# One decoder layer on one core: four score blocks placed one weight half later, and the first extraction placed inside a gate half

## The chip, the cores and the metric

The kernel runs on one core of a Trainium2 chip. The metric is the device time of one execution in microseconds (us), and less is better. Five engines work side by side, each through its own list of instructions in order: TensorE (PE; its weight loads are listed apart as PEld), VectorE (DVE), ScalarE (ACT), GpSimd (POOL) and SyncE (SP). They meet only through semaphores. SP and POOL also issue most of the transfers (DMA) from memory.

## The reference

One layer is computed for a prompt of 256 tokens and for 8 sample sequences of one token each, in float32, so that there are 264 columns of activations. In short:

```python
x = x + 0.5 * g1 * swiglu(mod1(rms_norm(x)))
proj = mod2(rms_norm(x)) @ w_in            # qA kA vA | qB kB vB | gA | gB
o_a = block-sparse attention, 8 heads x 64 (prompt, and samples over a paged cache of 1024 tokens)
o_b = differential attention, 4 heads, q/k halves of 64, value 128 (the same, with a second cache)
x = x + g2 * ((sigmoid(gA) * (o_a @ w_branch_moba) + sigmoid(gB) * (rms_norm(o_b) @ w_branch_diff)) @ w_out)
x = x + 0.5 * g3 * swiglu(mod3(rms_norm(x)))
```

The shifts, scales and gates (mod1 to mod3, g1 to g3) come from a product of a conditioning vector with `w_ada`. The new rows of keys and values are returned too.

## The kernel before

**Products.** Every float32 weight block of 1 MB lands in one of four slots `raw`. ACT cuts it into a high part `whi` (line 773), and DVE (line 1147) or POOL (line 723) computes the rest `wlo`. PE then runs three products for each 128 by 128 piece of weights: high by high, high by low, low by high, each over 264 columns. A block of 256 output columns is worked in two halves, and one half is 8 pieces, so 24 products. The halves of the key and value projection are numbered; `kv_product(u)` (lines 1729 to 1731) is half u. Halves 0 to 15 are keys and values, halves 16 to 19 are the first two gate blocks. The later gate blocks are worked by `gate_half` (lines 2103 to 2105), whose result lies in PSUM bank 3.

**Scores.** The sample queries need scores against two caches, A (moba) and B (diff). `scores(ab, u)` (line 2003) multiplies the queries with half a sequence of cache `ab`: 32 small matmuls. Before it, the half must have landed in a buffer (1 MB, four transfers, line 493; SP issues those of A, POOL those of B) and must have been transposed in place by DVE (`turn_keys`, line 1378). A buffer is free again when its scores are done. For B, load 15 goes where load 12 was, load 16 (already the values of the first sequence) where load 13 was, load 17 where 14 was and load 18 where 15 was. POOL works in this order, and waits at each load for the scores that free its buffer:

```python
for use in range(KVS + 2, 4 * TS):
    kv_load(pool, 1, use)
    ...
    if 11 <= use < POOL_HALVES - 1:
        lo(*filler(use))       # wlo of weight half `use`
```

**The loop over u on PE.** Step u does `kv_product(u)`, then turns earlier keys or values (`k_turn`, `k_back`, `v_turn`; a value half is turned by line 1938 after ACT has copied it to `vT`, line 940), then `scores(0, u + 2)` and `scores(1, u)`. DVE in the same order transposes the halves of both caches; behind the last of them, `turn_keys(1, 15)`, come the ranks of the first four sequences (`sample_ranks(0)`, lines 1435 to 1460), and on these waits the exponential on ACT (line 955). Behind that exponential ACT copies value half 15 for `v_turn` of step 16, and then cuts the weights of halves 18 and 19.

**After the loop.** PE does halves 17 to 19 and then eight steps c. In step c it multiplies the probabilities (`wpad`, written by ACT at line 1041) with the cached values (line 2138), turns the prompt's probabilities (line 2168), computes the next prompt scores (lines 2054 and 2055), and does the prompt's output (lines 2192 and 2193). In steps 1 to 6 there are two gate halves between these. After step 3 and after step 7 the sample outputs of four sequences are complete in banks 4 and 5. DVE masks them into `om` (line 1604), and PE extracts them: eight matmuls of `om` with the 4 columns of the constant `sel4` (line 2200). Each is recorded as two passes with a weight load of 128 by 128 each.

Of the kernel before, what the change touches and what calls it, by code (L numbers as in the profile page):

```python
# [23 lines left out]
P = 128  # L24
D = 1024
KC = D // P
TP = 256
TS = 8
# [15 lines left out]
ADAS = (NMOD * D + ADAW - 1) // ADAW  # L44
KVS = 3
GUEST_LAST = 8
FIRST_LAST = 10
GATE_GUEST = 18
BIG = 1e30
# [165 lines left out]
def build(nc, A, O):  # L215
    ctx = ExitStack()
    with ctx:
# [1503 lines left out]
        def _(pe):  # L1721
# [334 lines left out]

            for u in range(2 * TS + 1):
                kv_product(u)
                if 1 <= u < 17:
                    kind, i = kv_half(u - 1)  # L2060
                    if kind == "k":
                        k_sum(i)
                    else:
                        v_turn(u - 1, i)
                if 2 <= u < 18:
                    kind, i = kv_half(u - 2)
                    if kind == "k":
                        k_turn(u - 2, i)
                if 3 <= u < 19:
                    kind, i = kv_half(u - 3)  # L2070
                    if kind == "k":
                        k_back(i)
                if u == 5:
                    pe.wait_ge(s_nvar, 3)
                if u == 13:
                    pe.wait_ge(s_ecur, 1)
                    pe.wait_ge(s_kroot, 8)
                    for r4 in range(4):
                        ins = mm(bank[:, 4, r4:r4 + 1], ev0[:, r4, :], C("ones", 0, 1), start=True, stop=True)
                    ins.then_inc(s_cur, 1)  # L2080
                if u + 2 < 16:
                    scores(0, u + 2)
                if u < 16:
                    scores(1, u)
                if u == 11:
                    block_sums(0)
                if u == 14:
                    pe.wait_ge(s_knorm, 8)
                    pe.wait_ge(s_ncur, 1)
                    pe.wait_ge(s_part, 1)  # L2090
                    prompt_scores(0)
                if u == 16:
                    exp_sums(0)

            def gate_half(s, t):

                pe.wait_ge(s_sig, 2 * s - 2 + t)
                pe.wait_ge(s_lo, half_done(W_GATE + s, t))
                for k in range(KC):
                    wh = whi[s % 2][:, k * 256 + t * P:k * 256 + t * P + P]  # L2100
                    wl = wlo[s % 2][:, k * 256 + t * P:k * 256 + t * P + P]
                    out = bank[:, 3, GATE_COL:GATE_COL + T]
                    mm(out, wh, hhi[:, k, :], start=(k == 0), stop=False)  # L2103
                    mm(out, wh, hlo[:, k, :], start=False, stop=False)  # L2104
                    ins = mm(out, wl, hhi[:, k, :], start=False, stop=(k == KC - 1))  # L2105
                ins.then_inc(s_gemm, 1)
# [18 lines left out]
            for c in range(KC):  # L2125
# [50 lines left out]
                        pe.wait_ge(s_sig, 1)  # L2176
                    prompt_scores(c + 1)
                if gated:
                    gate_half(c + 1, 1)
                pe.wait_ge(s_pps, npp)  # L2180
                if c:
                    pe.wait_ge(s_pout, c)
# [9 lines left out]
                    mm(out[:, 0:TP], vtok[:, 0, v0:v0 + wd], pts[h][:, 0:256], start=True, stop=False)  # L2192
                    ins = mm(out[:, 128:TP], vtok[:, 1, v0:v0 + wd], pts[h][:, 256:384], start=False, stop=True)
                ins.then_inc(s_po, 1)
                if c % 4 == 3:

                    pe.wait_ge(s_om, c // 4 + 1)
                    for f in range(KC):
                        out = bank[:, 7, TS * f:TS * f + 4] if c == 3 else bank[:, 4 + f // 4, TS * (f % 4) + 4:TS * (f % 4) + 8]
                        ins = mm(out, om[:, f // 4, P * (f % 4):P * (f % 4) + P], C("sel4"), start=True, stop=True)  # L2200
                        if f == KC - 1 or (c > 3 and f == 3):
                            ins.then_inc(s_ext, 1)
            o_sum(KC - 1)
            pe.wait_ge(s_sig, 14)

# [75 lines left out]
```

## Time and profile before

| | |
|---|---|
| runs | 745.51, 746.17, 746.9 us; median 746.17 us |
| the profiled execution | 747.49 us; its span, from first to last instruction, is 745.8 us |
| PE busy | 722.3 us, 97% of the span |
| DVE, ACT, POOL busy | 464.2, 336.8, 135.7 us |
| granted TensorE clock, mean | 0.995 of full speed |
| DMA | 209.57 MB, mean 281 GB/s |

PE is busy when a matmul is running, whatever the clock at which it runs. A wait is idle time of an engine before an instruction, put down to the engine or the transfer that released it. The granted clock is 1.00 at 2.4 GHz and 0.50 at 1.2 GHz. Times in the timelines are counted from the start of the span.

### The profile page before, as it was taken

The numbers are of one execution on the slowest core, as the hardware profiler recorded it, in microseconds if no ns is written. First come the engines' busy times: TensorE is split into PE (matmuls) and PEld (weight loads), VectorE is DVE, ScalarE is ACT, GpSimd is POOL, SyncE is SP. The second block draws the span as 40 slices with busy tenths as digits, with TensorE's granted clock in tenths as the row PEclk, the third lists the DMA queues.
The fourth block names the chain that finished last, engine by engine and source line by source line (L and its number), as shares of the span: only waits on it lengthen the run. The fifth ranks groups of instructions, "written<-read, shape, count | busy, mean of one in ns | idle before, by whom it ended". The sixth has DMA issues, their size and how long they took to land.

```text
span 745.8 us, 17368 instructions
## 1 busy us (share of the span) xinstructions
PE 722.3 (97%) x6736; PEld 644.8 (86%) x6736; DVE 464.2 (62%) x696; ACT 336.8 (45%) x580; POOL 135.7 (18%) x233
## 2 busy tenths in 40 slices
PE   5899999999999999999989999999999999999998
PEld 2398898999999699999876766789979999999997
DVE  2564545446355779996998665788784555545442
ACT  1463343344254552554255553575564443444441
POOL 0100000002000422597994323210000000000000
PEclk9999999999999999999999999999999999999999
DMA  9977998996996988999999999996626555555531
GB/s 351 378 253 263 314 331 285 317 308 231 413 340 212 385 303 288 354 405 379 407 403 310 405 406 392 337 391 210 207 71 201 188 180 169 179 185 171 187 98 30
DMA packets 116794, 209.57 MB, mean 281 GB/s; under 512 B 6730, under 2 KB 100458, under 8 KB 104434
## 3 DMA queue, kind: packets, MB, share of 16 engines
q1 hardware_dynamic: 107040, 159.46, 61.8%
q0 software_dynamic: 9440, 49.04, 16.7%
q8 instruction: 47, 0.77, 0.4%
q14 instruction: 25, 0.20, 0.1%
q10 hardware_dynamic: 242, 0.11, 0.1%
HBM read 205.33 MB, written 3.24 MB: 280 GB/s over the span
## 4 chain that ended last, share of the span: by engine, by line
PE 76%; DMA 11%; DVE 5%; SPq 3%; issue 3%; ACT 2%; POOL 0%; POOLq 0%; DVEq 0%; ACTq 0%
PE bank L1729 20%; PE bank L1730 19%; PE bank L1731 19%; PE bank L2003 3%; PE bank L1785 3%; DMA early<-in_w_ada 3%; PE bank L2138 3%; DMA raw<-in_ffn_w_down 3%; DVE wlo L1147 2%; DMA raw<-in_w_in 2%; DMA kvA_lent<-in_cache_v_moba 2%; SPq L493 2%; PE bank L2103 1%; PE bank L2104 1%; PE bank L2105 1%
## 5 line engine op out<-in xcount | busy, mean ns | idle before, releaser
L1147 DVE TENSOR_TENSOR wlo<-raw,whi 128x1024 fp32r<-128x1024 f32 (+1 forms) x177 | 208.8, 1199 | 171.0 <-ACT whi L773 168.3
L1729 PE MATMUL bank<-hhi,whi 128*128 128x264 f32 x992 | 285.5, 288 | 2.9 <-POOL wlo L723 1.2
L1730 PE MATMUL bank<-hlo,whi 128*128 128x264 f32 x992 | 281.3, 284 | 0.0
L1731 PE MATMUL bank<-hhi,wlo 128*128 128x264 f32 x992 | 280.9, 283 | 0.0
L773 ACT ACTIVATE whi<-raw 128x1024 fp32r<-128x1024 f32 (+1 forms) x192 | 194.9, 1034 | 105.0 <-PE bank L1731 71.8
L1729 PEld LDWEIGHTS bank<-hhi,whi 128*128 128x128 f32 x992 | 186.8, 188 | 15.5 <-issue 14.3
L1730 PEld LDWEIGHTS bank<-hlo,whi 128*128 128x128 f32 x992 | 187.0, 188 | 0.0
L1731 PEld LDWEIGHTS bank<-hhi,wlo 128*128 128x128 f32 x992 | 186.1, 188 | 0.0
L1729 PE MATMUL bank<-ahi,whi 128*128 128x264 f32 x416 | 118.9, 286 | 1.0 <-DVE alo L1680 0.8
L1731 PE MATMUL bank<-ahi,wlo 128*128 128x264 f32 x416 | 118.2, 284 | 0.0
L1730 PE MATMUL bank<-alo,whi 128*128 128x264 f32 x416 | 117.6, 283 | 0.0
L1729 PEld LDWEIGHTS bank<-ahi,whi 128*128 128x128 f32 x416 | 78.3, 188 | 1.5 <-DVE alo L1680 1.0
L1730 PEld LDWEIGHTS bank<-alo,whi 128*128 128x128 f32 x416 | 78.3, 188 | 0.0
L1731 PEld LDWEIGHTS bank<-ahi,wlo 128*128 128x128 f32 x416 | 78.3, 188 | 0.0
L821 ACT ACTIVATE sil<-bank 128x528 f32<-128x528 f32 x22 | 13.5, 613 | 72.3 <-PE bank L1731 72.3
L723 POOL TENSOR_TENSOR wlo<-raw,whi 128x256 fp32r<-128x256 f32 x60 | 42.9, 745 | 8.2 <-ACT whi L773 6.4
L825 ACT ACTIVATE ahi<-act 128x528 f32 (+1 forms) x22 | 14.2, 645 | 53.7 <-DVE act L1221 53.7
L493 POOL DMA_DIRECT2D kvB<-in_cache_k_diff x36 | 19.1, 531 | 88.0 <-PE bank L1731 57.1
L493 POOL DMA_DIRECT2D kvB<-in_cache_v_diff x44 | 23.3, 531 | 42.2 <-PE bank L2138 27.5
L2103 PE MATMUL bank<-hhi,whi 128*128 128x264 f32 x96 | 28.6, 298 | 0.0
L1225 DVE TENSOR_TENSOR alo<-act,ahi 128x528 f32 (+1 forms) x22 | 15.6, 710 | 19.3 <-ACT ahi L825 19.3
L2104 PE MATMUL bank<-hlo,whi 128*128 128x264 f32 x96 | 27.3, 284 | 0.0
(305 smaller groups left out, 822.0 us busy)
## 6 DMA issues: line engine op xcount, KB each, us to landing
raw<-in_ffn_w_gate SPq DMA_DIRECT2D x22, 1024.0 KB, 5.4
raw<-in_ffn_w_up SPq DMA_DIRECT2D x22, 1024.0 KB, 5.5
raw<-in_w_ada SPq DMA_DIRECT2D x20, 1024.0 KB, 6.9
raw<-in_w_in SPq DMA_DIRECT2D x20, 1024.0 KB, 11.7
raw<-in_ffn_w_down SPq DMA_DIRECT2D x16, 1024.0 KB, 5.0
kvB<-in_cache_v_diff POOLq DMA_DIRECT2D x44, 256.0 KB, 6.3
kvA<-in_cache_v_moba SPq DMA_DIRECT2D x40, 256.0 KB, 7.6
kvA<-in_cache_k_moba SPq DMA_DIRECT2D x36, 256.0 KB, 6.6
```

The lines of the kernel that those rows point to most:

```text
L493: eng.dma_start(rows_, cache[bass.ds(page, 1)].rearrange("a (j t) d -> (a j) (t d)", t=4)).then_inc(kv_sem(ab, use), 16)
L723: ins = nc.gpsimd.tensor_tensor(low[:, k:k + 2, :], full[:, k:k + 2, :], high[:, k:k + 2, :], ALU.subtract)
L773: nc.scalar.activation(half_view(whi[key[1] % 2], key, t), half_view(raw[s], key, t), ACT.Copy).then_inc(s_hi, 1)
L1147: dve.tensor_tensor(half_view(wlo[key[1] % 2], key, t), half_view(raw[s], key, t), half_view(whi[key[1] % 2], key, t).bitcast(F32), ALU.su ...
L1729: mm(out, wh, xh, start=start, stop=False)
L1730: mm(out, wh, xl, start=False, stop=False)
L1731: return mm(out, wl, xh, start=False, stop=stop)
L1785: ins = mm(bank[32 * j:32 * j + 32, b, 0:n].rearrange("p (t a) -> p t a", a=32), csilu[:, kc, :], cols[:, :, j, :], start=(kc == 0), stop= ...
L2003: ins = mm(bank[32 * m:32 * m + 32, b6, c0:c0 + 128].rearrange("p (q c) -> p q c", q=4), qrow[s % 2][:, 16 * ab + 4 * m + b, :], kv_slot(a ...
L2103: mm(out, wh, hhi[:, k, :], start=(k == 0), stop=False)
L2104: mm(out, wh, hlo[:, k, :], start=False, stop=False)
L2138: ins = mm(bank[32 * q:32 * q + 32, 4 + ab, :], wpad[half][:, q, ab, w0:w0 + 32], kv_slot(ab, use)[:, q, :], start=(half == 0 and c % 4 == ...
```

## The change

Two orders on PE are changed; no computation is added or left out. `scores(1, u)` for u = 12 to 15 is done one step later, directly behind `kv_product(u + 1)` and ahead of the turning. The eight extraction matmuls of step 3 move from behind the prompt's output of step 3 into the gate half just ahead of it: two go ahead of each of the last four weight pieces of that half. The waits for `om` (`s_om`) and for ACT's copies of the turned probabilities (`s_pps`, all eight so far) move with them. The extraction of step 7 stays where it was.

```diff
+LATE_B = 12
...
             for u in range(2 * TS + 1):
                 kv_product(u)
+                if u > LATE_B:
+                    scores(1, u - 1)
...
                 if u + 2 < 16:
                     scores(0, u + 2)
-                if u < 16:
+                if u < LATE_B:
                     scores(1, u)
...
-            def gate_half(s, t):
+            def extract(c, f):
+
+                out = bank[:, 7, TS * f:TS * f + 4] if c == 3 else bank[:, 4 + f // 4, TS * (f % 4) + 4:TS * (f % 4) + 8]
+                ins = mm(out, om[:, f // 4, P * (f % 4):P * (f % 4) + P], C("sel4"), start=True, stop=True)
+                if f == KC - 1 or (c > 3 and f == 3):
+                    ins.then_inc(s_ext, 1)
+
+            def gate_half(s, t, c=None):
...
                 for k in range(KC):
+                    if c is not None and k == 4:
+                        pe.wait_ge(s_om, c // 4 + 1)
+                        pe.wait_ge(s_pps, 2 * (c + 1))
+                    if c is not None and k >= 4:
+                        extract(c, 2 * (k - 4))
+                        extract(c, 2 * (k - 4) + 1)
...
                 if gated:
-                    gate_half(c + 1, 1)
+                    gate_half(c + 1, 1, c if c == 3 else None)
...
-                if c % 4 == 3:
-
+                if c == KC - 1:
                     pe.wait_ge(s_om, c // 4 + 1)
                     for f in range(KC):
-                        out = bank[:, 7, TS * f:TS * f + 4] if c == 3 else bank[:, 4 + f // 4, TS * (f % 4) + 4:TS * (f % 4) + 8]
-                        ins = mm(out, om[:, f // 4, P * (f % 4):P * (f % 4) + P], C("sel4"), start=True, stop=True)
-                        if f == KC - 1 or (c > 3 and f == 3):
-                            ins.then_inc(s_ext, 1)
+                        extract(c, f)
```

## Rows read from the trace of the kernel before

**Rows 1.** The page, busy time of each engine (share of the span) and instructions

```profile
PE 722.3 (97%) x6736; PEld 644.8 (86%) x6736; DVE 464.2 (62%) x696; ACT 336.8 (45%) x580; POOL 135.7 (18%) x233
```

**Rows 2.** Waits of PE over the whole span: total us, times, longest

```profile
PE bank L1938 <- ACT vT L940: 1.8, 1, 1.8
...
PE bank L1729 <- POOL wlo L723: 1.2, 1, 1.2
...
PE bank L2138 <- ACT wpad L1041: 0.4, 1, 0.4
```

**Rows 3.** Timeline of PE, steps 11 to 13: start us, duration us, instructions

```profile
354.30 1.08 PE L2003 MATMUL bank<-kvA,qrow 128*32 128x128 f32 x32
355.20 1.06 PE L2003 MATMUL bank<-kvB_lent,qrow 128*32 128x128 f32 x32
...
359.86 1.08 PE L2003 MATMUL bank<-kvA_lent,qrow 128*32 128x128 f32 x32
361.61 1.08 PE L2003 MATMUL bank<-kvB,qrow 128*32 128x128 f32 x32 [0.67 <-DVE kvB L1378]
362.62 0.39 PE L1729 MATMUL bank<-hhi,whi 128*128 128x264 f32 x1
...
365.63 0.38 PE L1938 MATMUL bank<-const,vT 128*128 128x128 f32 x2
...
366.84 1.08 PE L2003 MATMUL bank<-kvA,qrow 128*32 128x128 f32 x32
368.39 1.08 PE L2003 MATMUL bank<-kvB,qrow 128*32 128x128 f32 x32 [0.47 <-DVE kvB L1378]
```

**Rows 4.** Timeline of ACT, exponential, value half 15, gate weights, probabilities

```profile
382.59 0.51 ACT L955 ACTIVATE prob<-prob,mxt 128x256 f32<-128x256 f32 x1 [6.88 <-DVE ncur L1460]
...
383.68 0.37 ACT L940 ACTIVATE vT<-bank 128x264 f32<-128x264 f32 x1
...
393.91 2.01 ACT L773 ACTIVATE whi<-raw 128x1024 fp32r<-128x1024 f32 x2 [4.51 <-DMA raw<-in_w_in]
...
396.58 0.40 ACT L1041 ACTIVATE wpad<-probT 128x64 f32<-128x64 f32 x2
```

**Rows 5.** Timeline of DVE, last transpose of B and end of the ranks

```profile
373.52 2.31 DVE L1378 STREAM_TRANSPOSE kvB<-kvB 128x2048 f32<-128x2048 f32 x1 [1.55 <-DMA kvB<-in_cache_k_diff]
...
382.40 0.16 DVE L1460 TENSOR_TENSOR ncur<-ncur,mxt 128x2 f32<-128x2 f32 x1
```

**Rows 6.** Timeline of POOL, loads 15 and 16 of B, wlo of halves 16 and 18

```profile
364.08 2.14 POOL L493 DMA_DIRECT2D kvB<-in_cache_k_diff  x4
...
370.15 1.69 POOL L493 DMA_DIRECT2D kvB<-in_cache_v_diff  x3 [1.11 <-PE bank L2003]
...
372.75 2.82 POOL L723 TENSOR_TENSOR wlo<-raw,whi 128x256 fp32r<-128x256 f32 x4
...
385.56 3.28 POOL L723 TENSOR_TENSOR wlo<-raw,whi 128x256 fp32r<-128x256 f32 x4 [1.41 <-issue]
```

**Rows 7.** DMA issues of 345 to 348.5 us, then of 364 to 366.4 us: median us to landing

```profile
kvB<-in_cache_k_diff POOLq DMA_DIRECT2D x4, 256.0 KB, 5.8
...
kvB<-in_cache_k_diff POOLq DMA_DIRECT2D x4, 256.0 KB, 6.6
```

**Rows 8.** Stretches: length; busy us (x instructions) of PE, PEld, DVE, ACT, POOL; PE's clock; DMA share; GB/s

```profile
26.50:28.90 2.40, 0.00 (x0) 0.00 (x0) 2.40 (x8) 0.00 (x0) 0.00 (x0) 0.97 0.99 336
28.90:30.00 1.10, 1.09 (x8) 0.20 (x8) 0.23 (x2) 0.00 (x0) 0.00 (x0) 0.50 1.09 348
...
382.10:384.10 2.00, 0.22 (x2) 0.00 (x1) 1.83 (x8) 1.51 (x7) 2.00 (x4) 1.00 0.98 393
...
451.57:453.42 1.85, 1.85 (x17) 0.41 (x16) 0.00 (x0) 0.39 (x1) 0.21 (x1) 1.00 1.03 419
444.96:448.36 3.40, 3.40 (x18) 0.59 (x17) 2.57 (x4) 1.30 (x2) 0.00 (x0) 0.53 1.01 419
443.08:444.96 1.88, 1.88 (x18) 1.86 (x17) 1.23 (x5) 1.88 (x7) 0.00 (x0) 1.00 0.99 409
```

## Prediction, written before the changed kernel was run

> **What bounds the kernel now.** I read the page first: PE is busy 97% of the span [rows 1], so a change of order can win only where PE waits or where it runs slowly. Then I read the list of PE's waits [rows 2], the timelines of PE, ACT, DVE and POOL around steps 11 to 16 [rows 3 to 6], and last a table of stretches with the granted clock [rows 8]. The reader should see three things. First, steps 12 and 13 each have a hole between the scores of cache A and those of cache B. Second, the same part of the loop is followed by other waits, 1.8 us for value half 15, 1.2 us for the low part of half 18 and 0.4 us for the first `wpad` [rows 2]. Third, the clock falls to half behind the first extraction.
>
> **Part 1, the late scores: what they remove.** In an undisturbed step the B scores start 0.90 us behind the A scores (354.30 to 355.20). In step 12 it is 1.75 us (359.86 to 361.61), in step 13 1.55 us (366.84 to 368.39) [rows 3]. So 0.85 + 0.65 = 1.50 us of waiting for DVE's transpose goes away: a whole product half of 3.01 us (362.62 to 365.63) now lies ahead of these scores.
>
> **What they set later.** The scores of step 12 free the buffer of load 15. Before, they ended at 361.61 + 1.08 = 362.69. After, half 13 starts at 359.86 + 1.01 = 360.87 (1.01 is the distance from a score block to the next half, 361.61 to 362.62), the late scores start 3.01 later at 363.88 and end at 364.96 [rows 3]. POOL needed 0.68 us from the end of such scores to its first transfer (368.39 + 1.08 = 369.47, then 370.15) [rows 3, 6]. It would start load 15 at 365.64 instead of 364.08, which is 1.56 us later [rows 6].
>
> DVE had nothing else to do and waited 1.55 us for this very load at 373.52 [rows 5]. Behind its transpose come the ranks, which end at 382.56, the exponential at 382.59 and, in ACT's order, the copy of value half 15 at 383.68 [rows 4, 5], and for that copy PE waits in step 16. So the holes are removed ahead of a wait whose end does not come from PE's pace: the 1.50 us move into it, and the wait ends later by what the load lands later. Call that X. Its upper bound is the whole 1.56 us. Its lower bound is near 0: the four pieces of load 15 took 6.6 us to land in the median against 5.8 for a load issued behind a pause of the queue [rows 7], so up to 0.8 us of a later issue may be hidden in the queue. I take X = 1.0, nearer to 1.56 − 0.8 = 0.76 than to 1.56.
>
> **What is late next.** Behind that copy ACT cuts half 18, and POOL forms its low part at 385.56, after 1.41 us of idling [rows 6]. POOL has a second way to be late. The scores of step 13 now run behind half 14, and I place them so: late scores of step 12 at 363.88, plus 1.01; turning and own products, 365.63 to 366.84, 1.21; scores of A, 1.01; half 14, 3.01; together 370.1, end 371.2, against 369.47 before [rows 3]. Load 16 starts at 371.9 instead of 370.15, and the low part of half 16 behind it at 374.5 instead of 372.75 [rows 6], 1.75 us later. POOL then works without a pause up to its idle 1.41 us, so it would be ready for half 18 0.35 us later than before. Half 16 itself would be wanted by PE at about that time, but what PE loses there lies ahead of the wait for value half 15. Product 18 thus starts later by the larger of X and 0.35, so by 1.0.
>
> Behind half 19 PE had waited 0.42 us for `wpad`. That one does not move: ACT had waited 4.51 us for the gate weights at 393.91, and `wpad` followed at 396.58 [rows 4]. These weights are a transfer of SP, whose waits look at cache A alone. So 0.4 of the 1.0 us is covered, and part 1 costs 0.6 us. Its bounds are 0 (X up to 0.4) and 1.56 − 0.4 = 1.15 us. No row lets part 1 win: the last wait of the stretch ends by a transfer.
>
> **The clock behind the longer wait.** The wait for value half 15 was 1.8 us and the clock stayed at 1.00 through 382.10 to 384.10 [rows 8]. It grows by 1.5 + X minus small losses ahead of it, to some 3.5 to 4 us. Early in the kernel PE stood still from 26.50 to 28.90, 2.4 us, and ran the next products at 0.50, which is 1.2 GHz [rows 8]. So I expect half 17 to begin at 1.2 GHz. At half speed it could take up to 3 us more, but it has cover: the wait for half 18 behind it, 1.2 us. A slow stretch as long as the 3.40 us at 0.53 [rows 8] loses about 1.6 us, so 0 to 0.6 us may come out of the cover. I take 0.1, as a part of such a stretch falls into the idle time itself.
>
> **Part 2, the extraction.** From 443.08 to 444.96 PE did 16 passes of 4 columns, 1.88 us, 0.117 us for each weight load. The clock was still at 1.00, and then fell: the 16 value products behind them took 3.40 us at 0.53, against 1.85 us for the same 16 at 451.57 [rows 8]. That is 1.55 us lost. With wide products between the extractions the engine never streams so little for so long, and I take the 1.55 us as won. The 16 loads stay. Of four passes ahead of a weight piece the first load can hide behind the wide product before it, but the load of the next wide product then has no wide one to hide behind, so nothing is won in the count. For four switches between the two kinds I add 0.1 us (bounds 0 and 0.5, one exposed load of 0.117 for each). The two waits that moved cost nothing: `om` was masked right behind the sample's last product, ahead of that gate half, and `s_pps` waits for copies that ACT makes ahead of it too. If that cover were gone, the masking of two blocks on DVE would be the price, in which the gate half would stand. The prompt's output of step 3 moves back by 1.9 us and what ACT does behind it too, but the gate weights cut there are wanted two steps later.
>
> The Trainium skill speaks of both things. "TensorE: Matmul & The Clock Gate", What's actually happening, says that the throttled state is the default and that activity releases it. By that the fall behind the 4-column passes and behind a longer stand-still are of one kind, and the trace agrees (0.53 and 0.50). The same page, in Step-by-step, says that TensorE's queue pulls weight loads ahead of running matmuls. Taken at its widest, the extraction's loads would vanish between the products; the rival below gives the price from rows.
>
> **The sum.** Part 1 +0.6, the clock behind the wait +0.1, part 2 −1.55 + 0.1 = −1.45. Together −0.75 us. The profiled execution took 747.49 us with a span of 745.8, so it becomes 746.7 with a span of 745.0. It lies 1.3 us above the median of the runs, 746.17, and from that median I get **745.4 us**, 0.1% less. About 0.2% (1.5 us) is what a measurement of this kernel can tell from no change, so I call this the same.
>
> **Rivals.**
> 1. *Load 15 is not delayed* (X at most 0.4), because the queue was full anyway. For it speaks 6.6 against 5.8 us [rows 7], against it that DVE waited for exactly this load [rows 5]. Part 1 costs 0, the sum is −1.45: 744.7 us. Chance 0.17.
> 2. *The clock gain isn't there*: it falls within the interleaved stretch as well, or did not fall in the timed runs. For it speaks that the stretch holds 12 wide products among 16 loads of 1.88 us, so it is less than half wide, and that the profiled run is slower than all three others; against it that the wide products are spread evenly. The sum is +0.6 + 0.1 + 0.1 = +0.8: 747.0 us. Chance 0.17.
> 3. *The other side: the stand-still ahead of step 16's turning throttles the clock past its cover.* It is the longest wait behind the start, and one slow stretch costs 1.6 us. From 0.75 us uncovered on, the change is slower than before; with the full 1.6 it is +0.75: 746.9 us, and with X at its upper bound 747.5. Against it stands the cover of 1.2 us. Chance 0.08.
> 4. *The extraction's loads hide* behind the wide products (the pull-ahead of the page above). With 3 in 4 hidden, 1.4 us more is won: 744.0 us. The pace of 0.117 us per load in the 4-column passes [rows 8] speaks against it, since there too nothing else held the loads. Chance 0.06.
> 5. *The 1.50 us are kept*, as the ranks or the gate weights come earlier with the transfers that now stand aside. The sum is −1.5 − 1.45: 743.2 us. Against it stand rows 4 and 5. Chance 0.08.
>
> **How the numbers follow.** My own case has 0.44, with 744.8 to 746.3 as its own range. Faster by over 0.2% means below 744.7: rivals 4 and 5, 0.4 of rival 1 and a tail of mine, together 0.24. Slower means above 747.7: tails of rivals 2 and 3, 0.06. The same is left with 0.70. The range of 8 in 10 leaves out rival 5, half of rival 4 and the far ends of rivals 2 and 3: 743.9 to 747.3 us.
>
> **What would show it.** In the changed kernel's timeline the two waits of line 2003 for line 1378 are gone. The first transfer of load 15 starts near 365.6, DVE's last transpose of B near 374.5, and PE's wait for `vT` (line 940) is 3.5 us or more. The low part of half 18 starts near 386.5, the wait for `wpad` is gone, and the first value product starts near 397.5. In the stretch behind the extraction the clock is 1.00 and 16 value products take 1.85 us. I am wrong if the wait for `vT` stays under 2.5 us, if `wpad` comes earlier than 396.5, or if the value products behind the extraction still take over 3 us.

## The result, and the profile after

The changed kernel takes **750.36 us** (median of 5 runs, 748.79 to 751.3) against 746.39 us of the kernel before (5 runs, 745.51 to 746.9). The ratio is 1.005 with a 95% interval of 1.0036 to 1.0064: it is slower by 4.0 us. I had forecast 745.4 us, between 743.9 and 747.3. So the sign was wrong, and the time lies outside the range. In a second comparison the changed kernel took 750.27 us against 746.34.

The profiled execution of the changed kernel took 748.79 us with a span of 747.1. Line numbers are one higher than before up to line 2055 (line 1378 is now 1379, 723 is 724), and the value products of line 2138 are now line 2154.

The page, busy time of each engine (answers to [rows 1]):

```profile
PE 721.9 (97%) x6736; PEld 646.5 (87%) x6736; DVE 469.2 (63%) x696; ACT 337.4 (45%) x580; POOL 135.5 (18%) x233
```

The waits of PE over the whole span (total us, times, longest; answers to [rows 2]):

```profile
PE bank L1939 <- ACT vT L941: 4.1, 1, 4.1
...
PE bank L1730 <- DVE wlo L1148: 2.0, 3, 1.3
PE bank L2055 <- issue: 2.0, 1, 2.0
```

The two waits of step 12 and 13 for DVE's transpose are gone, as the change wants. So are the waits for the low part of half 18 and for `wpad`. But the one wait for value half 15 has grown from 1.8 to 4.1 us, and a wait of 2.0 us that was not there before stands in step 14. PE's busy total is 0.4 us lower. It counts slow products as busy too, so it mixes the slow stretch of [rows 8] that is gone with a new one, below.

The timeline of PE (answers to [rows 3], and on to step 4 behind the loop):

```profile
359.02 1.08 PE L2004 MATMUL bank<-kvA_lent,qrow 128*32 128x128 f32 x32
...
363.14 1.08 PE L2004 MATMUL bank<-kvB,qrow 128*32 128x128 f32 x32
...
373.06 0.50 PE L2055 MATMUL bank<-kT,qT 64*128 64x128 f32 x4 [1.98 <-issue]
...
386.61 0.69 PE L1939 MATMUL bank<-const,vT 128*128 128x128 f32 x2 [4.12 <-ACT vT L941]
...
388.17 0.42 PE L1732 MATMUL bank<-hhi,wlo 128*128 128x264 f32 x1
...
394.19 0.28 PE L1732 MATMUL bank<-hhi,wlo 128*128 128x264 f32 x1
...
399.84 1.06 PE L2154 MATMUL bank<-kvA,wpad 128*32 128x512 f32 x8
...
443.73 0.50 PE L2101 MATMUL bank<-const,om 128*128 128x4 f32 x4
...
447.88 1.06 PE L2154 MATMUL bank<-kvA_lent,wpad 128*32 128x512 f32 x8
```

The late scores of step 12 start 4.12 us behind the scores of A (359.02 to 363.14); before it was 1.75. Most products of half 17 are 0.22 us apart (0.42 us each), those of half 18 0.12 us apart.

The timeline of POOL, loads 15 and 17 and the low parts of halves 17 and 18 (answers to [rows 6]):

```profile
364.92 2.28 POOL L494 DMA_DIRECT2D kvB<-in_cache_k_diff  x4 [1.62 <-PE bank L2004]
...
378.80 2.28 POOL L494 DMA_DIRECT2D kvB_lent<-in_cache_v_diff  x4 [0.88 <-PE bank L2004]
381.11 2.78 POOL L724 TENSOR_TENSOR wlo<-raw,whi 128x256 fp32r<-128x256 f32 x4
...
388.06 3.26 POOL L724 TENSOR_TENSOR wlo<-raw,whi 128x256 fp32r<-128x256 f32 x4 [1.98 <-issue]
```

Load 17 and the low part of half 17 in the trace of before, for comparison:

```profile
376.78 2.15 POOL L493 DMA_DIRECT2D kvB_lent<-in_cache_v_diff  x4
378.95 3.12 POOL L723 TENSOR_TENSOR wlo<-raw,whi 128x256 fp32r<-128x256 f32 x4
```

Load 17 now waits 0.88 us for the late scores of step 14, and the low part of half 17 behind it starts 3.0 us later than before (22.09 against 19.09 us behind the scores of A of step 12).

The DMA issues of 364.5 to 367.3 us, median us to landing (answers to [rows 7]):

```profile
kvB<-in_cache_k_diff POOLq DMA_DIRECT2D x4, 256.0 KB, 6.9
```

The timeline of DVE, the last transpose of B and the ranks (answers to [rows 5]):

```profile
366.91 3.19 DVE L1367 TENSOR_TENSOR qroot<-qroot,const 128x32 f32<-128x32 f32 x1
...
375.48 2.31 DVE L1379 STREAM_TRANSPOSE kvB<-kvB 128x2048 f32<-128x2048 f32 x1 [2.52 <-DMA kvB<-in_cache_k_diff]
...
381.12 2.79 DVE L1456 TENSOR_TENSOR mxt<-mxt,ncur 128x2 f32<-128x2 f32 x1
...
384.90 0.16 DVE L1461 TENSOR_TENSOR ncur<-ncur,mxt 128x2 f32<-128x2 f32 x1
```

DVE's idle time ahead of this transpose has grown from 1.55 to 2.52 us. Line 1367 (1366 before) took 0.5 us in the trace of before, and 3.19 here, beside POOL's low part of half 15 (367.22 to 370.03), which sets back the copy of `ncur` (372.84) for which PE waits 2.0 us in step 14. The timeline of ACT (answers to [rows 4]):

```profile
385.09 0.51 ACT L956 ACTIVATE prob<-prob,mxt 128x256 f32<-128x256 f32 x1 [11.19 <-DVE ncur L1461]
...
386.19 0.37 ACT L941 ACTIVATE vT<-bank 128x264 f32<-128x264 f32 x1
...
397.41 0.40 ACT L1042 ACTIVATE wpad<-probT 128x64 f32<-128x64 f32 x2
```

The first `wpad` is written from 397.41 on, 0.83 us later than in [rows 4] (1.67 us when the traces are laid on the scores of A of step 12), as ACT now waits for PE there and no longer for the gate weights. PE wants it only at 399.84. So the path from ranks to half 18 sets the end of the stretch, with no cover by the gate weights left. The windows (columns as in [rows 8]; the last three are PE's clock, the DMA share and GB/s):

```profile
384.50:386.60 2.10, 0.00 (x0) 0.00 (x0) 1.93 (x8) 1.51 (x7) 1.51 (x3) 0.63 1.01 379
386.60:391.60 5.00, 4.99 (x23) 4.92 (x24) 4.72 (x13) 4.81 (x14) 3.37 (x5) 0.50 1.06 384
391.60:395.41 3.81, 3.81 (x32) 3.76 (x30) 3.67 (x10) 2.51 (x3) 3.81 (x6) 0.96 0.45 151
443.73:446.53 2.80, 2.80 (x27) 2.80 (x26) 2.38 (x10) 2.04 (x7) 0.00 (x0) 1.00 1.07 403
447.88:449.73 1.85, 1.85 (x18) 0.41 (x16) 0.49 (x2) 1.73 (x3) 0.00 (x0) 1.00 1.03 426
```

The clock fell to 0.50 behind the wait of 4.12 us and stayed there for some 5 us of products. Behind the extraction it is at 1.00, and the 16 value products take 1.85 us.

**Where the time went.** I lay both traces on the start of the scores of A in step 12 and follow the chain (us behind that start). "Before again" is a second trace of the kernel before, "again" a second one of the changed kernel; both were taken with the experiments.

| | load 15 issued | last transpose starts | ranks end | `v_turn` of half 15 | behind half 18 | first value product |
|---|---|---|---|---|---|---|
| before | 4.22 | 13.66 | 22.70 | 24.25 | 32.20 | 37.03 |
| before again | 4.22 | 13.24 | 23.25 | 24.80 | 32.85 | 37.19 |
| changed | 5.90 | 16.46 | 26.04 | 27.59 | 36.48 | 40.82 |
| changed again | 5.89 | 17.05 | 26.04 | 27.58 | 36.55 | 40.89 |

The first value product comes 3.79 us later: 1.68 from the issue of load 15, 1.12 more until its transpose starts (2.80 so far), 0.54 more until the ranks end, 0.94 more over halves 17 and 18, and 0.49 given back in what follows. That is near the loss of the medians. Each of these parts is the difference of two single traces. Between the second traces of both kernels the first value product comes 3.70 us later, but in other parts: the transpose 3.81 later, the ranks' end only 2.79, 0.91 more over halves 17 and 18, and nothing given back. So the total holds, and its split does not.

**The ranks' end does not follow the transpose.** In the two traces of the changed kernel the transpose starts 0.59 us apart (16.46 and 17.05), and the ranks end at the same 26.04. What lies at the same place in both is POOL's low part of half 17, from 22.09 to 24.87. A rank operation that meets it ends with it, and behind that the same 1.15 us of operations follow. From the second trace, VectorE and then GpSimd:

```profile
377.48 2.31 DVE L1379 STREAM_TRANSPOSE kvB<-kvB 128x2048 f32<-128x2048 f32 x1 [3.11 <-DMA kvB<-in_cache_k_diff]
...
383.12 2.21 DVE L1456 TENSOR_TENSOR mxt<-mxt,ncur 128x2 f32<-128x2 f32 x1
...
382.52 2.78 POOL L724 TENSOR_TENSOR wlo<-raw,whi 128x256 fp32r<-128x256 f32 x4
```

In two experiments below with the same score order, the transpose starts at 16.62 and 15.91. There a rank operation ends at 24.88 and 24.89, and the ranks at 26.02 and 25.33 (in the last it is a later operation that meets the block, so fewer are left). So over a range of 1.14 us of transpose starts the block sets the end. Line 1456 takes 0.16 us undisturbed, so without the block the ranks of the first trace would end at 26.04 − 2.63 = 23.41, an estimate. The start of the document says that the engines meet only through semaphores; here VectorE and GpSimd also meet without one.

The two profiled executions differ less, 747.1 against 745.8 us of span, because that trace of before held the slow stretch of [rows 8] behind the extraction. From the first value product to the second set of value products of step 4 it took 54.68 us, against 52.99 in the changed kernel and 52.70 in the second trace of before.

### The profile page after: what moved, and what is told of

Read it like the earlier page. It is cut to its first block, busy times and chain, and to the rows that moved or that the text cites. A ratio compares the mean times of both kernels' runs of the same rounds, so it can differ in the third digit from the quotient of the medians.

```text
span 747.1 us, 17369 instructions
## 1 busy us (share of the span) xinstructions
PE 721.9 (97%) x6736; PEld 646.5 (87%) x6736; DVE 469.2 (63%) x696; ACT 337.4 (45%) x580; POOL 135.5 (18%) x233
## 4 chain that ended last, share of the span: by engine, by line
PE 79%; DVE 8%; DMA 7%; issue 3%; ACT 2%; SPq 0%; POOL 0%; POOLq 0%; ACTq 0%; DVEq 0%
PE bank L1730 20%; PE bank L1731 19%; PE bank L1732 19%; PE bank L1786 4%; PE bank L2004 4%; DMA raw<-in_ffn_w_down 3%; PE bank L2154 3%; DVE wlo L1148 3%; DMA kvA_lent<-in_cache_v_moba 2%; PE bank L2119 1%; DMA kvB<-in_cache_k_diff 1%; PE bank L2120 1%; PE bank L2121 1%; DMA crow<-in_c_rows 1%; ACT whi L774 1%
## 6 DMA issues: line engine op xcount, KB each, us to landing
raw<-in_w_in SPq DMA_DIRECT2D x20, 1024.0 KB, 10.1
```

## The experiments

Each kernel ran on a chip together with others and with the kernel before. Positions below 50 us are again counted from the start of the scores of A in step 12, larger ones from the start of the span. Diffs are against the changed kernel unless said otherwise.

### Each part alone

*Late scores only*: the extraction is put back behind the prompt's output.

```diff
-                if c == KC - 1:
+                if c % 4 == 3:
...
-                    gate_half(c + 1, 1, c if c == 3 else None)
+                    gate_half(c + 1, 1)
```

> The late scores alone; the extraction stays where it was. In the changed kernel's trace the first value product of the late steps came 2.95 us later than before (399.84 against 396.89), while the stretch from there to the value products behind the extraction took the same, and those took 1.85 instead of 3.40 us. Theory A: the late scores carry the whole loss and the interleaving wins 1.5 us, so this kernel is the slowest of all: 746.4 + 5.5, about 752 us, and its value products behind the extraction take 3.4 us at half clock. Theory B, a rival: the clock behind the extraction falls in few executions, so the interleaving is worth nothing in the median, and this kernel takes the same as the changed one, 750.4 us.

*Interleaving only* (against the kernel before): the score order is the old one.

```diff
-                    gate_half(c + 1, 1)
+                    gate_half(c + 1, 1, c if c == 3 else None)
...
-                if c % 4 == 3:
+                if c == KC - 1:
```

> The interleaved extraction alone; the scores stay in their old steps. Theory A: 746.4 - 1.5 = 744.9 us, waits of steps 12, 13 and 16 as before. Theory B: 746.4 us, no change. A third theory, that the interleaving itself costs (its outputs of step 3 are 1.9 us later for ACT), gives over 747 us.

Beside 746.28 us of before (25 runs), the late scores alone take 749.14 us (6 runs; 1.0039, interval 1.0024 to 1.0055), the interleaving alone 746.11 us (12 runs; 0.9995, interval 0.9984 to 1.0006). The loss belongs to the late scores. The interleaving does not win the 1.45 us that I gave it, and costs nothing either. The trace with late scores only also shows why it wins nothing. Its windows around the extraction in a row, then behind the wait for half 15:

```profile
446.34:448.21 1.87, 1.87 (x18) 1.86 (x16) 1.22 (x5) 1.87 (x7) 0.00 (x0) 1.00 1.04 433
448.21:450.06 1.85, 1.85 (x17) 0.42 (x16) 1.50 (x3) 1.30 (x2) 0.00 (x0) 1.00 1.01 416
...
386.08:388.00 1.92, 1.92 (x9) 1.84 (x10) 1.82 (x6) 1.92 (x6) 0.64 (x2) 0.50 1.07 354
```

Here the same 16 passes stand in a row, and the 16 value products behind them take 1.85 us at 1.00, where [rows 8] have 3.40 us at 0.53. The fall behind the extraction is something that happens in some executions. In three traces with the eight extractions in a row I saw it once; with them interleaved, in none of nine. That is too few to say whether it is rarer there. The 78 executions of the kernel before in these comparisons have mean clocks from 1.00 (13 of them, median 745.8 us) to 0.993 (10 of them, 747.6 us). So executions differ by 1.8 us with their clock, but the median one can't have paid 1.55 us in this place, or the interleaving alone would be that much faster than it. Nor does a low mean clock point to this place: the second trace of before has 0.993 and no fall here.

The sum of the two parts alone, +2.86 − 0.17 = +2.7 us, is 1.2 us short of the +3.9 to +4.0 of the whole change. The executions with late scores only lie between 748.65 and 750.26 us, those of the changed kernel between 748.21 and 751.35. Whether the rest is an interaction or the spread of few runs stays open.

### Load 15 on time

*The scores of step 12 stay where they were*, those of 13 to 15 are late.

```diff
-LATE_B = 12
+LATE_B = 13
```

> As the changed kernel, but the late order begins one step later, so that the scores of step 12 are in their old place and load 15 of cache B is issued as before; loads 16 to 18 are still late. Theory A1, load 15 carries the loss (DVE's last transpose, ranks, exponential, value half 15): the wait for vT falls from 4.1 to about 2.5 us (as the hole of step 13 still moves into it), the clock holds, and the time is that of the interleaving alone or up to 0.5 us more, 745 to 745.5 us. Theory A2, the loss comes from POOL's late low parts and its later collisions with DVE: at least half of the loss stays, 748 us or more.

748.49 us (12 runs; 1.0029, interval 1.0017 to 1.0042). Load 15 is issued at 4.20, its transpose starts at 13.37, both as before. Yet more than half of the loss stays, so the late load is not the whole cause. The trace shows the rest behind the transpose:

```profile
374.98 2.53 DVE L1443 TENSOR_TENSOR rank<-sm 128x32 f32<-128x32 f32 x1
...
381.15 1.80 DVE L1456 TENSOR_TENSOR mxt<-mxt,ncur 128x2 f32<-128x2 f32 x1
```

These two take 0.19 and 0.16 us where they run undisturbed. In the same trace POOL works on low parts:

```profile
374.64 2.80 POOL L724 TENSOR_TENSOR wlo<-raw,whi 128x256 fp32r<-128x256 f32 x4
...
380.82 2.78 POOL L724 TENSOR_TENSOR wlo<-raw,whi 128x256 fp32r<-128x256 f32 x4
```

DVE's first one ends 0.07 us behind POOL's block (374.98 + 2.53 = 377.51, and 374.64 + 2.80 = 377.44), the second inside the next block, at 382.95. From the transpose's start to the ranks' end it took 11.5 us, against 9.0 and 10.0 in the two traces of before. The late scores of step 13 make load 16 late on POOL, and the low part of half 16 behind it then falls on the ranks. The first value product comes at 38.84, 1.7 to 1.8 us late. This trace is of one of the fastest executions of the kernel (746.6 us, 1.9 below its median), so it shows where time is lost, and not all that the median loses.

The Trainium skill, "SBUF — State Buffer", Who interferes with whom, says that a VectorE instruction with two inputs in SBUF contends with a GpSimd instruction that reads SBUF. The trace agrees: both stretched ones are tensor-tensor operations of that kind, and in the changed kernel line 1456 took 2.79 us from 381.12 on beside a low part from 381.11 to 383.89.

### The stand-still filled

*Four idle products on PE ahead of the wait of step 16*, into a bank that nothing reads, so that PE does not stand still so long. They wait for the copies of an earlier value half, so that they don't run ahead.

```diff
+FILL = 4
...
+                if u == 16:
+                    pe.wait_ge(s_vtok, 2 * (kv_half(13)[1] + 1))
+                    idle_products(1, FILL)
```

> As the changed kernel, with four products of constants into a free bank ahead of the turning of value half 15 in step 16, so that TensorE isn't still there (they take about 3.5 us of the 4.1 us wait; their result is used by nobody). In the changed kernel half 17 ran at 0.50 until 391.6, and two halves took 7.8 us against 6.0 at full clock. If the fallen clock is part of the loss, this kernel is 1.5 to 2 us faster than the changed one, 748.5 us, with the clock at 1.00 from 386 to 392. If the waits behind it (the low part of half 18 at about 388.1 + 3.3 = 391.4, against 390.6 where half 17 would end at full clock) take the gain back, it is 1 us faster at most. If the clock fell for another reason, no change.

748.72 us (8 runs; 1.0032, interval 1.002 to 1.0044). The wait for value half 15 is 0.5 us now, the clock is 1.00 through 382 to 394, and `v_turn` starts at 27.57 as in the changed kernel, but half 18 is done at 35.53 instead of 36.48. So the clock behind the stand-still costs the 0.94 us of the table in these traces, and 1.55 to 1.6 us in the medians. Where the other 0.6 us come from is not shown. The wait of 1.2 us for the low part of half 18 is back in this trace, so the late ranks had not drawn on that cover; the slow clock had used it up. The clock is a part of the loss, and not the larger one.

### The ranks ahead of the last transpose

*DVE does the ranks before it waits for load 15.* They read nothing of load 15.

```diff
+                if u == 14:
+                    v.wait_ge(s_ncur, 1)
+                    sample_ranks(0)
                 if u + 1 < 16:
                     turn_keys(1, u + 1)
```

> As the changed kernel, but VectorE does the ranks of the first four sequences ahead of the last transpose of cache B, so that they no longer wait for load 15. They can start at about 373.0 and end at 373 + 9.6 - 2.3, about 380.2; value half 15 is copied at about 381.4, before TensorE wants it at 382.4. Theory A, the loss is the chain from load 15: the wait for vT is under 0.5 us, the clock holds. What is late next is POOL: load 18 waits for the last scores (issued until 386.1), so the low part of half 18 starts near 386.1 instead of 388.1 and product 18 near 389.5; the first value product near 397.5 instead of 399.8. Time 2.3 us and the clock's 1.8 us less than the changed kernel, partly the same microseconds: 747 to 748 us. If collisions of VectorE with POOL carry the loss by themselves, the ranks take as long as before wherever they stand and the gain is the same as long as they end by 382; so the wait for vT is the test of the chain and e7 that of the collisions.

*The same, and POOL forms the low parts of halves 18 and 19 ahead of load 18.*

```diff
             for use in range(KVS + 2, 4 * TS):
+                if use == POOL_HALVES - 2:
+                    lo(*filler(use))
+                    lo(*filler(use + 1))
                 kv_load(pool, 1, use)
```

> As e5, and POOL forms the low parts of halves 18 and 19 ahead of load 18 instead of behind it. Theory: POOL is then ready near 384, half 18 follows half 17 without a wait (start near 385.5), half 19 ends near 392, and the first wpad is the last wait: its gate weights land near 393.9 and wpad follows near 396.5, so that TensorE idles about 4 us there. First value product near 396.6, time 745 to 746 us, no better than the kernel before by more than 0.5 us, because the transfer of the gate weights bounds this stretch. If the transfers aren't the bound, up to 3 us better: 743 us.

Beside 746.34 us of before (24 runs), the first takes 748.72 us (6 runs; 1.0028, interval 1.0016 to 1.004), the second 746.9 us (12 runs; 1.0005, interval 0.9996 to 1.0014), with the late scores left in. The waits of PE for the first:

```profile
PE bank L1730 <- POOL wlo L724: 2.3, 1, 2.3
PE bank L2055 <- issue: 2.0, 1, 2.0
PE bank L2004 <- DVE kvB L1379: 1.5, 1, 1.5
```

The wait for `vT` is gone, which shows that the ranks' place behind load 15 sets it. This does not part the late load from POOL's low part of half 17, as the ranks now end at 21.65, ahead of both. They meet the low part of half 16 instead, where one operation takes 3.12 us. What is late next is POOL: it forms the low part of half 18 behind load 18, whose buffer the later scores of step 15 free. With that turned round too, the whole loss but 0.6 us is gone, and the rest is within the noise. The expectation of 745 to 746 us was missed: PE does not wait for `wpad` there. The waits then:

```profile
PE bank L2056 <- issue: 2.0, 1, 2.0
PE bank L2005 <- DVE kvB L1380: 1.5, 1, 1.5
...
PE bank L2036 <- DVE prob L1429: 1.0, 1, 1.0
```

All but the first name DVE, and the first ends right behind its copy of `ncur`: by these waits DVE now bounds the stretch. Here too a rank operation is stretched, beside POOL's low part of 374.10 to 376.92:

```profile
373.86 3.12 DVE L1446 TENSOR_TENSOR rank<-rank,const 128x32 f32<-128x32 f32 x1
```

*The same again, with only the scores of step 15 late.*

```diff
-LATE_B = 12
+LATE_B = 15
```

> As e6 (ranks ahead of the last B transpose, low parts of halves 18 and 19 ahead of load 18), but only the scores of step 15 are late, so that loads 15 to 17 go out as before. Theory, VectorE is nearly full in this stretch (36.6 of 40 us busy in 360 to 400 before), so that any order of TensorE's work ends up waiting for it: the waits of steps 12 and 13 stay, those of step 16 and of half 18 shrink, the transpose of load 15 ends near 382 and its scores wait about 1 us; 745.5 to 746.5 us, the same as before or up to 0.8 us better. If the order of TensorE were what matters, e6, with less in its way, would have been better than this one: then 747 us.

746.54 us (11 runs; 1.0001, interval 0.999 to 1.0012) beside 746.21 of before (29 runs). With the ranks first, the score order hardly matters, 746.9 or 746.5 on two chips. The new order of DVE and POOL wins nothing measurable with either of them. The waits for the transposes, 4.7 us in three pieces, are back in place of what it saves:

```profile
PE bank L2005 <- DVE kvB L1380: 4.7, 3, 2.9
```

### POOL's blocks taken away from the ranks

*POOL forms only the first quarter of the low parts of halves 14 to 17*; the other three quarters of these four low parts are left out.

```diff
-                for k in range(0, KC, 2):
+                short = 2 if n == W_KV + 7 or (n, t) in ((W_GATE, 0), (W_GATE, 1)) else KC
+                for k in range(0, short, 2):
```

> As the changed kernel, but POOL computes only the first quarter of the low parts of halves 14 to 17 (the rest keeps old contents; this part of the computation is left out). In the traces so far a tiny VectorE operation stretches from 0.2 to 2.5 to 3.2 us when it falls on a POOL low part. Theory of collisions: the stretch from the last B transpose to the end of the ranks falls from 9.6 to about 7 us (with POOL's transfer issues still in it), and the time by 1.5 to 2.5 us, to 748 to 749 us, more if the wait gets short enough for the clock to hold. Rival: the operations are stretched by something else, or load 15 alone matters: the ranks still take 9 us and the time stays within 0.5 us of the changed kernel.

*The changed kernel itself*, on the same chip:

> The changed kernel itself, beside the other three on the same chip, for its time and a second trace: 750.4 us, with the last B transpose 16 to 17 us behind the A scores of step 12, PE's wait for vT near 4 us or more, and half 17 at 0.50.

747.54 us (12 runs; 1.0018, interval 1.0002 to 1.0035) against 750.27 us (6 runs; 1.0042, interval 1.003 to 1.0055). 2.7 us of the loss of 3.9 go away. The transpose of load 15 starts at 17.06, as in the changed kernel again (17.05), and yet the ranks end at 24.97 instead of 26.04. So 1.07 us of the ranks' end is POOL's block and not the load. Half 18 was done at 34.53 instead of 36.55. The wait for `vT` is 5.1 us there, so a long stand-still alone doesn't make the loss. Two things are mixed in this kernel, though: the ranks are less disturbed, and POOL reaches load 17 and half 18 earlier. So for the time the kernel bounds what POOL's work in this stretch costs in all, and does not part the two. With the blocks cut short the ranks still end 1.7 to 2.3 us later than in the two traces of before (22.70 and 23.25): the late load is felt as well once the block is out of its way.

### How much the extraction itself costs

*Seven of the eight extraction matmuls of step 3 left out*, the eighth in its old place (against the kernel before).

```diff
-                    for f in range(KC):
+                    for f in (range(KC) if c > 3 else (KC - 1,)):
```

> The kernel before, with seven of the eight extraction matmuls of step 3 left out (this part of the computation is missing; the eighth stays in its place). 14 passes of 0.117 us go, 1.64 us. Theory A, the clock falls behind the extraction in every execution and takes 1.55 us more: 1.64 + 1.55 = 3.2 us faster than before, 743.1 us. Theory B, it falls in a few executions: 1.6 to 2.2 us faster, 744.1 to 744.7 us. The value products of step 4 take 1.85 us either way.

*The same seven left out of the interleaved form* (against the kernel with the interleaving only).

```diff
-                    if c is not None and k >= 4:
-                        extract(c, 2 * (k - 4))
-                        extract(c, 2 * (k - 4) + 1)
+                    if c is not None and k == 7:
+                        extract(c, KC - 1)
```

> As e2 (interleaved extraction, scores in their old steps), with seven of the eight extraction matmuls of step 3 left out (this part is missing), the eighth ahead of the last weight piece of the gate half. Against e2 (746.1 us, no different from before) it shows what the interleaved ones cost: 1.64 us if each load is paid between the products too, so 744.5 us; 0.4 us, so 745.7 us, if three in four of the loads hide behind wide products. Against e9 it shows whether the place of the one extraction matters: no.

*The kernel before again*, for its trace:

> The kernel before, one look for a second trace of the stretch behind the extraction. Theory A: the value products of step 4 take 3.4 us at 0.53 again. Theory B: in this execution they may take 1.85 us at 1.00; then the fall isn't a property of the order but of the execution.

Beside 746.21 us of before, seven extractions fewer give 744.76 us in a row (12 runs; 0.9979, interval 0.9967 to 0.999) and 744.77 us interleaved (11 runs, and one more of 2182 us left out; 0.9985, interval 0.9972 to 0.9997). So the seven cost 1.45 us in a row, and 746.11 − 744.77 = 1.3 us interleaved, from runs on two chips whose intervals are some 1 us wide to either side. 14 passes by 0.117 us would be 1.64. The trace of the changed kernel is sharper: the gate half with eight extractions in it took 442.17 to 447.07, 4.90 us, against 3.10 us for the gate half ahead of it. So the 16 passes cost 1.80 us there, and 1.88 in a row. Were the weight loads hidden between wide products, they would cost far less.

The second trace of before ran at 746.11 us. Its wait for `vT` is 2.35 us, and the clock behind that:

```profile
386.00:390.00 4.00, 4.00 (x23) 4.00 (x22) 3.76 (x10) 3.86 (x12) 3.31 (x5) 0.58 1.02 397
```

Before, a wait of 1.79 us was followed by 1.00, this one of 2.35 us by 0.58. With one extraction in the old place, 2.35 us of waiting was followed by 1.00:

```profile
384.70:388.00 3.30, 3.30 (x28) 3.28 (x29) 3.09 (x10) 3.30 (x9) 1.88 (x3) 1.00 1.05 410
```

With one extraction interleaved, 2.33 us was followed by 0.50 again (386 to 388 us). So whether the clock falls behind a stand-still of this length differs from trace to trace, in the kernel before as well. A wait of 2.91 us, for the last transpose with only the scores of step 15 late, was followed by 1.00, and one of 2.79 us, with the interleaving only, by 0.50. Behind waits of 3.4 to 5.1 us it fell in all five traces that have one.

## Why the prediction was wrong

**Part 1, what is removed: right, and worth nothing, as said.** The 1.50 us of waits are gone and went into the wait for `vT`, which is 4.12 us; I had 3.5 to 4.

**The ranks at a fixed distance behind load 15, and "its upper bound is the whole 1.56 us": this step failed.** X was the time by which PE's wait for value half 15 ends later. I took 1.0 us; `v_turn` of half 15 starts 3.3 us later in the first pair of traces and 2.8 in the second. The step failed in two places.

*The load.* The issue of load 15 came 1.68 us later, near the 1.56 that I worked out. But its transpose started 2.80 us later than in the profiled trace of before, and 3.4 in the second trace of the changed kernel. I had asked only how much of the delay the queue might hide, and not whether a load issued later might also take longer. Over the traces, the time from the first issue to the transpose is 9.0 to 10.1 us where load 15 is on time (six traces) and 10.0 to 11.2 where it is late (five). The median to landing explains 0.3 of it (6.6 to 6.9 us), the four issues 0.14 (2.14 to 2.28 us). The DMA engines were at a share of 1.0 in both. What makes the last piece land later still is not settled.

*The ranks.* I let them follow the transpose at a fixed distance, and so took load 15 for what sets their end. In all four traces with this score order POOL's low part of half 17 sets it. From the transpose's start to their end it took 9.0 and 10.0 us in the two traces of before, 9.6 and 9.0 in those of the changed kernel, 7.9 with three quarters of POOL's work on these low parts away, and would take 6.95 if no operation were stretched (9.58 − 2.63, an estimate). So the collision was there before too; what is new is that the block has moved back with the ranks. I had asked of POOL only whether it is ready for half 18, with a delay of 1.75 us and no pause up to its idle 1.41. But it pauses once more, 0.88 us for the scores of step 14, and the low part of half 17 is 3.0 us late. With load 15 on time the ranks take 11.5 us, 1.5 to 2.5 more than before, and the trace shows no other loss of that size.

**The wait of 2.0 us in step 14: not in my account, and free.** It stands ahead of the wait for `vT`, which is shorter by it. Where the ranks come first it is one of the waits that are left.

**"I take 0.1" for the clock behind the longer wait: mis-sized.** The fall came, as predicted, and with it the 0.50. It cost 0.94 us over halves 17 and 18 in the traces, and filling the stand-still won 1.6 us in the medians. My cover was the wait for half 18, 1.2 us. It was used up: the wait is gone, and the two halves took 7.8 us (387.59 to 395.41) against 6.0 at full clock. I had reckoned with a slow stretch of 3.4 us; here some 5 us of products ran slow. This is rival 3, with the size it named (up to 1.6 us), and I had given it 0.08. In the second trace of before the clock fell too, and there the cover nearly held: from `v_turn` to the end of half 18 it took 8.05 us, against 7.95 in the first trace and 8.9 in the changed kernel.

**Part 2, "I take the 1.55 us as won": failed, as rival 2 said.** The fall behind the extraction was one execution's, and I had noted that the profiled run was slower than the three others. I still took it out of the median. Measured, part 2 wins 0.2 us by the medians, and by the interval it lies between 1.2 us won and 0.4 lost. The clock at 1.00 and the 1.85 us behind the extraction, which I named as the test, came true and prove nothing, since with the extraction in a row they stand in two traces of three as well. Rival 4 is refuted by the 1.80 us that the 16 interleaved passes take in the trace.

**The cover of 0.42 us for `wpad`: right for the profiled trace.** The wait is gone, and 0.49 us was given back there. That `wpad` does not move was wrong, without harm. The second trace of before has no such wait, and nothing was given back against it, so this cover too belongs to single executions.

**The sum again.** With the sizes of the first pair of traces it is +3.34 (X: transpose 2.80, ranks 0.54) + 0.94 (clock) − 0.49 (`wpad`) = +3.8 for part 1 and −0.2 for part 2, +3.6, against +4.0 and +3.9 measured for the whole. Late scores alone measured +2.9, which is 0.9 less than that sum. In the second pair it is +2.79 (X) + 0.91 (clock) = +3.7 for part 1. From rival 3 with X at its bound (747.5) to the result it is 2.9 us. X passed its bound by 1.2 to 1.8, and part 2 fell short of its 1.45 by 1.25; together 2.5 to 3.0. Rivals 1 and 5 are refuted by the table: load 15 was delayed, and nothing of the 1.50 us was kept.

**The tests that I named.** First transfer of load 15 near 365.6: 364.92, where the whole trace runs 0.84 us ahead at step 12. Last transpose near 374.5: 375.48. Low part of half 18 near 386.5: 388.06. First value product near 397.5: 399.84. The waits and the clock that I had named as signs came out as named, the wait for `vT` of over 3.5 us among them, and none of the three signs of being wrong appeared, while the forecast failed: none of them looked at what sets the ranks' end. How far each of these times lies behind its forecast grows along the chain, and that pattern, not the single values, shows which terms were too small.

No kernel tried beats the kernel before by more than the measurement tells, except those that leave work out.

## What to carry to other kernels

When a consumer is moved back to remove a wait, look for what its end frees; if an engine further on already waits for that transfer, the delay of its issue is no upper bound of the cost. The transfer may be slower, and what follows it may meet another engine's work, whose place has moved too. To see which of them sets an end, compare traces in which one has moved: if the end stays, it is the other. A slow stretch of the clock seen in one profile belongs to that execution: before its end is booked as a gain, look at a second trace or at whether the profiled run lies above the median by that much. A cover is spent once, and it has a size: here the throttled clock alone took 2.1 us from `v_turn` to the end of half 18 (8.89 us, against 7.95 − 1.20 without the wait), and 1.2 us were covered.

## What the hardware showed that I had not expected

- Small VectorE operations of 0.16 to 0.19 us took 1.8 to 3.2 us when they met a block of four GpSimd tensor operations, and mostly ended with the block, not with its first operation (381.12 + 2.79 = 383.91 against the block's end at 383.89). With late scores only, even a tensor-scalar operation on 128x32 did so, 2.66 us at 381.43 beside a block of 381.27 to 384.05. Before, the collision was spread over three or four operations instead, and cost 2.1 and 3.1 us in the two traces, against 2.6 and 2.0 in the changed kernel.
- The clock behind a wait for `vT` of 2.3 to 2.4 us fell to 0.50 within 2 us or so in two traces and stayed at 1.00 in a third, and behind the same 16 passes of 4 columns 0.53 in one and 1.00 in two.
- Loading weights for a 4-column pass costs nearly its 0.117 us between wide products too: 1.80 us for 16 passes, in the trace of the changed kernel.
